# The first stage of layer 0 in another order: X first, modulation blocks in pairs, six projection tiles abreast

## The reference, cut to what matters

```python
mod_l = jnp.split((jax.nn.silu(c) @ ada_w[l] + ada_b[l])[:, None, :], 6, axis=-1)
mod_c = jnp.split(jax.nn.silu(c_ctx) @ ada_w[l] + ada_b[l], 6, axis=-1)
hl = modulate(rmsnorm(xl, norm_mix_pre[l]), mod_l[0], mod_l[1])   # h * (1 + scale) + shift
hc = modulate(rmsnorm(xc, norm_mix_pre[l]), mod_c[0], mod_c[1])
zl = hl @ w_in[l]
zc = hc @ w_in[l]
```

## Time and profile before

| | us |
|---|---|
| median of three runs | 1781.99 (1780.87 to 1786.96) |
| profiled execution | 1783.33 |
| its span | 1781.5 |
| TensorE busy | 1616.1 (91%) |
| VectorE busy | 913.7 (51%) |
| ScalarE busy | 783.3 (44%) |
| GpSimd busy | 302.2 (17%) |

### The profile page before, as it was taken

How to read it: one execution, slowest core, us unless ns; L and a number is a source line. 1 busy time by engine, 2 the same in 40 slices (tenths; PEclk the granted TensorE clock), 3 DMA queues, 4 the chain that set the end, 5 groups by cost and what they waited for, 6 DMA issues and landing times.

```text
span 1781.5 us, 35712 instructions
## 1 busy us (share of the span) xinstructions
PE 1616.1 (91%) x15480; PEld 1325.9 (74%) x15480; DVE 913.7 (51%) x1435; ACT 783.3 (44%) x1286; POOL 302.2 (17%) x241
## 2 busy tenths in 40 slices
PE   3799999977689999799999999899988789979997
PEld 1588767766566668488888886887876678979997
DVE  0444355466335433655555224655676436567754
ACT  1532355564225233634434323624765344565653
POOL 1023023512010000011112100131441110002210
PEclk9799999999899999899999999999999999989999
DMA  8742255504385212123222634734513275425554
GB/s 238 215 145 95 93 180 171 163 17 144 98 269 168 85 47 95 48 95 95 95 95 80 118 96 150 219 120 137 165 58 121 51 256 171 143 95 178 184 159 120
DMA packets 230347, 234.67 MB, mean 132 GB/s; under 512 B 5872, under 2 KB 217072, under 8 KB 230064
## 3 DMA queue, kind: packets, MB, share of 16 engines
q1 hardware_dynamic: 210560, 190.17, 34.0%
q0 software_dynamic: 15024, 35.92, 7.3%
q10 hardware_dynamic: 4608, 6.29, 1.1%
HBM read 216.63 MB, written 15.73 MB: 130 GB/s over the span
## 4 chain that ended last, share of the span: by engine, by line
PE 64%; DVE 5%; issue 5%; ACT 4%; DMA 1%; POOL 0%; ACTq 0%; DVEq 0%; POOLq 0%
PE ps L1792 15%; PE ps L1793 15%; PE ps L1794 15%; PE ps L2136 4%; PE ps L1994 2%; PE ps L1981 2%; PE ps L2033 1%; DVE wlo L1254 1%; PE ps L1830 1%; DVE X L1321 1%; ACT whi L849 1%; PE ps L1955 1%; PE ps L1815 1%; PE ps L1944 1%; DMA ring<-in_ffn_up 1%
## 5 line engine op out<-in xcount | busy, mean ns | idle before, releaser
L849 ACT ACTIVATE whi<-ring 128x1024 fp32r<-128x1024 f32 (+1 forms) x264 | 275.6, 1046 | 566.5 <-PE ps L1794 505.6
L1254 DVE TENSOR_TENSOR wlo<-ring,whi 128x1024 fp32r<-128x1024 f32 (+1 forms) x264 | 327.5, 1244 | 228.3 <-ACT whi L849 227.4
L1792 PE MATMUL ps<-H,whi 128*128 128x512 f32 (+1 forms) x656 | 220.8, 337 | 2.4 <-DVE wlo L1254 2.4
L1793 PE MATMUL ps<-H,whi 128*128 128x512 f32 (+1 forms) x656 | 220.6, 336 | 0.0
L1794 PE MATMUL ps<-H,wlo 128*128 128x512 f32 (+1 forms) x656 | 220.6, 336 | 0.0
L1792 PE MATMUL ps<-HR,whi 128*128 128x512 f32 (+1 forms) x592 | 211.6, 357 | 2.2 <-DVE wlo L1254 1.8
L1794 PE MATMUL ps<-HR,wlo 128*128 128x512 f32 (+1 forms) x592 | 207.7, 351 | 0.0
L1793 PE MATMUL ps<-HR,whi 128*128 128x512 f32 (+1 forms) x592 | 207.7, 351 | 0.0
L1792 PEld LDWEIGHTS ps<-H,whi 128*128 128x128 f32 x656 | 124.6, 190 | 16.0 <-issue 3.2
L1793 PEld LDWEIGHTS ps<-H,whi 128*128 128x128 f32 x656 | 124.6, 190 | 12.7
L1794 PEld LDWEIGHTS ps<-H,wlo 128*128 128x128 f32 x656 | 124.6, 190 | 12.7
(11 more groups left out here) (307 smaller groups left out, 3043.3 us busy)
## 6 DMA issues: line engine op xcount, KB each, us to landing
ring<-in_ada_w SPq DMA_DIRECT2D x48, 1024.0 KB, 5.8
ring<-in_ffn_up SPq DMA_DIRECT2D x44, 1024.0 KB, 5.1
ring<-in_w_gate SPq DMA_DIRECT2D x32, 1024.0 KB, 6.9
ring<-in_w_in SPq DMA_DIRECT2D x24, 1024.0 KB, 5.3
ring<-in_ffn_down SPq DMA_DIRECT2D x32, 512.0 KB, 3.8
WB<-in_w_branch POOLq DMA_DIRECT2D x8, 1024.0 KB, 7.9
ring<-in_w_o SPq DMA_DIRECT2D x8, 1024.0 KB, 5.2
ring<-in_ffn_down SPq DMA_DIRECT2D x16, 384.0 KB, 4.0
```

What stands on the lines that cost most here:

```text
L849: act.activation(whi[:, m % SPLIT, 0:kn, :], ring[:, SLOT[raw] % RING, 0:kn, P * half:P * half + P], ACT.Copy).then_inc(hi_done, 1)
L1254: dve.tensor_tensor(wlo[:, m % SPLIT, 0:kn, :], ring[:, SLOT[raw] % RING, 0:kn, P * half:P * half + P], whi[:, m % SPLIT, 0:kn, :].bitcast ...
L1792: pe.matmul(o[:, c0:c1], hi[:, i, :], part(0, k), start=(k == 0), stop=False)
L1793: pe.matmul(o[:, c0:c1], hi[:, i, :], part(1, k), start=False, stop=False)
```

## The change

- **DMA order.** SP issues c, the first 130 columns of the constants (the ones and `fold`, which now lead the table), X in two halves, modulation blocks 0 and 4, the vectors, three slots of input weights, then blocks 1, 5, 2, 6, 3, 7, then the rest of the constants, and from there on the input weights as before. The eight blocks of the first stage no longer go through `ring`: they have four slots of their own (`ada`) in a part of `Z` that is not used yet. The fifth to eighth of them wait until PE has used the block that lay in their slot.
- **Modulation in pairs.** The jobs are placed by pair: blocks q and 4 + q, then their two transposes, for q = 0 to 3. Pair 0 stands in front of the sum of squares; pairs 1 to 3 stand between the products. DVE makes the gain of two row tiles (`first_gain`) as soon as the pair is there.
- **Six tiles abreast.** `whi` and `wlo` have six slots for the first six tiles of `z`. PE goes over the six tiles for k = 0 and 1, then does pair 1, then k = 2 and 3, and so on; the last two `k` are done tile by tile.
- **ACT and DVE** follow the same order: squares before the first fill, two weight halves, the rows of pair 0, the other four halves, then pair by pair. DVE multiplies all eight row tiles by the root at the first pair. The small vectors and the bias table's addition come after the last pair.
- **Banks.** `NCON_EARLY` is 130, `FIRST` 6, `FIRST_SLOTS` 4. The jobs in front of the first `z` job use banks 6 and 7 in turn, and the counting of banks starts at the first `z` job.

```diff
--- before
+++ after
...
+MOD_FIRST_ORDER = [n for q in range(4) for n in (q, 4 + q)]
...
-    first = modulation_jobs(MOD_FIRST)
-    plan = {("start", 0, 0): first[:5], ("start", 0, 1): first[5:]}
+    plan = {}
+    for q in range(4):
+        pair = [(0, q), (0, 4 + q)]
+        plan["start", 0, q] = [(kind,) + b for kind in ("mod", "modt") for b in pair]
...
     for l in range(LAYERS):
-        jobs += FILL.get(("start", l, 0), []) + [("ss", l, 0)] + FILL.get(("start", l, 1), [])
+        jobs += FILL.get(("start", l, 0), []) + [("ss", l, 0)]
+        for q in range(1, 4):
+            jobs += FILL.get(("start", l, q), [])
         for n, t in enumerate(Z_ORDER):
...
+    early = list(JOB)[:JOB["z", 0, Z_ORDER[0]]]
+    for name in early:
+        k = NBANK - 2 + JOB[name] % 2
+        place[name] = k
+        needs[name] = {owner[k]} - {None}
+        count[k] += 1
+        release[name] = owner[k] = (k, count[k])
...
+        if name in place:
+            continue
...
+        if (l, job[2]) in MOD_FIRST:
+            return []
...
+def half_slot(m):
+    return m if m < FIRST else m % SPLIT
...
+def half_before(m):
+    return m - FIRST if m < FIRST + SPLIT else m - SPLIT
...
-        whi = at("whi", 132, [SPLIT, KT, P], F32R)
-        wlo = at("wlo", 144, [SPLIT, KT, P], F32R)
+        whi_at = [132, 136, 140, 112, 116, 120]
+        wlo_at = [144, 148, 152, 156, 160, 164]
+        whi = [at(f"whi{n}", whi_at[n], [KT, P], F32R) for n in range(FIRST)]
+        wlo = [at(f"wlo{n}", wlo_at[n], [KT, P], F32R) for n in range(FIRST)]
+        ada = at("ada", 48, [FIRST_SLOTS, KT, SLOT_N])
...
+        x_in = [sem("x_in0"), sem("x_in1")]
...
+        ada_in = [sem(f"ada_in{i}") for i in range(FIRST_SLOTS)]
...
         def _(sp):
+            def ada_first(n):
+                o = MOD_FIRST_ORDER.index(n)
+                if o >= FIRST_SLOTS:
+                    sp.wait_ge(mm_done, done_at(("mod", 0, MOD_FIRST_ORDER[o - FIRST_SLOTS])))
+                sp.dma_start(ada[:, o % FIRST_SLOTS, :, :],
+                             a["ada_w"][0, :, n * SLOT_N:(n + 1) * SLOT_N].rearrange("(k p) n -> p k n", p=P))\
+                  .then_inc(ada_in[o % FIRST_SLOTS], 16)
...
+            sp.dma_start(con[:, 0:NCON_EARLY], a["const"][:, 0:NCON_EARLY]).then_inc(const_early, 16)
+            for x in range(2):
+                sp.dma_start(X[:, 4 * x:4 * x + 4, :],
+                             a["xin"][512 * x:512 * x + 512, :].rearrange("(k p) t -> p k t", p=P)).then_inc(x_in[x], 16)
+            ada_first(0)
+            ada_first(4)
+            sp.dma_start(vec[:, :].rearrange("p (l n) -> p l n", l=LAYERS),
+                         a["vecs"].rearrange("l p n -> p l n")).then_inc(vec_in, 16)
...
-                if n == 1:
...
-                    sp.dma_start(con[:, :], a["const"]).then_inc(const_in, 16)
-                if n == 3:
-                    sp.dma_start(X[:, :, :], a["xin"].rearrange("(k p) t -> p k t", p=P)).then_inc(x_in, 16)
-                    sp.dma_start(vec[:, :].rearrange("p (l n) -> p l n", l=LAYERS),
-                                 a["vecs"].rearrange("l p n -> p l n")).then_inc(vec_in, 16)
+                if n == FIRST // 2:
+                    for q in range(1, 4):
+                        ada_first(q)
+                        ada_first(4 + q)
+                    sp.dma_start(con[:, NCON_EARLY:NCON], a["const"][:, NCON_EARLY:NCON]).then_inc(const_in, 16)
...
-                    if m >= SPLIT:
...
-                        old = HALVES[m - SPLIT][0]
+                    if m >= FIRST:
...
+                        old = HALVES[half_before(m)][0]
...
-                            act.wait_ge(mm_done, done_at(HALF_JOB[m - SPLIT]))
...
+                            act.wait_ge(mm_done, done_at(HALF_JOB[half_before(m)]))
...
             def norm_finish(l, k, src, dst):
...
-                act.wait_ge(gains_ready, 2 * l + 1 + k // 2)
+                act.wait_ge(gains_ready, 2 * l + k // 2)
...
-            fill(("start", 0, 0))
-            act.wait_ge(x_in, 16)
...
+                act.wait_ge(x_in[i // 4], 16)
...
+            fill(("start", 0, 0))
...
-            fill(("start", 0, 1))
+            split_until(2)
...
+            def first_rows(i):
+                act.wait_ge(first_gain, i // 2 + 1)
+                act.wait_ge(h_half, i + 1)
+                for x in range(2):
+                    v = Z[:, i, 256 * x:256 * x + 256]
+                    ins = act.activation(v, v, ACT.Identity, bias=mod[:, 0, i, x:x + 1], scale=amod[:, 0, i, x:x + 1])
+                ins.then_inc(h_full, 1)
...
+            def first_high(i):
+                act.wait_ge(h_full, i + 1)
+                act.activation(HR[:, 0, i, :], Z[:, i, :], ACT.Copy).then_inc(h_hi, 1)
...
+            for q in range(4):
+                if q:
+                    fill(("start", 0, q))
+                first_rows(2 * q)
+                first_rows(2 * q + 1)
+                first_high(2 * q)
+                first_high(2 * q + 1)
+                if q == 0:
+                    split_until(FIRST)
             for l in range(LAYERS):
...
-                split_until(half_no(("z", l, Z_ORDER[0])) + SPLIT)
                 if l:
+                    split_until(half_no(("z", l, Z_ORDER[0])) + SPLIT)
...
-                norm_finish(l, 0, Z, HR)
+                    norm_finish(l, 0, Z, HR)
...
                 for n, t in enumerate(Z_ORDER):
...
-                    split_until(half_no(("z", l, t)) + 1 + SPLIT)
+                    split_until(half_no(("z", l, t)) + 1 + (FIRST if l == 0 and n < SPLIT else SPLIT))
...
-                    if (l, k) != (0, 0):
-                        over_rms(l, k, src, tmp, i)
+                    over_rms(l, k, src, tmp, i)
...
-            dve.wait_ge(x_in, 16)
-            for i in range(KT):
-                over_rms(0, 0, X, Z, i)
+            def first_low(i):
+                dve.wait_ge(h_hi, i + 1)
+                dve.tensor_tensor(HR[:, 1, i, :], Z[:, i, :], HR[:, 0, i, :].bitcast(F32), ALU.subtract).then_inc(h_ready, 1)
...
+            for x in range(2):
+                dve.wait_ge(x_in[x], 16)
+            dve.wait_ge(vec_in, 16)
+            for q in range(4):
+                fill(("start", 0, q))
+                gb = vc(0, "mix_pre", 2 * q, 2).unsqueeze(2).to_broadcast([P, 2, 2])
+                for n in (q, 4 + q):
+                    emptied(dve, ("modt", 0, n))
+                dve.scalar_tensor_tensor(amod[:, 0, 2 * q:2 * q + 2, :], mod[:, 0, 8 + 2 * q:10 + 2 * q, :], 1.0, gb,
+                                         ALU.add, ALU.mult).then_inc(first_gain, 1)
+                if q == 0:
+                    for i in range(KT):
+                        over_rms(0, 0, X, Z, i)
+                    split_until(2)
+                first_low(2 * q)
+                first_low(2 * q + 1)
+                if q == 0:
+                    split_until(FIRST)
...
-            dve.wait_ge(vec_in, 16)
             for l in range(LAYERS):
...
-                if l == 0:
-                    fill(("start", 0, 0))
-                    fill(("start", 0, 1))
-                gains(l, (0,))
+                if l:
+                    gains(l, (0,))
...
-                split_until(half_no(("z", l, Z_ORDER[0])) + SPLIT)
-                norm_apply(l, 0, X, Z, HR)
+                if l:
+                    split_until(half_no(("z", l, Z_ORDER[0])) + SPLIT)
+                    norm_apply(l, 0, X, Z, HR)
...
                 for n, t in enumerate(Z_ORDER):
-                    split_until(half_no(("z", l, t)) + SPLIT)
+                    split_until(half_no(("z", l, t)) + (FIRST if l == 0 and n < SPLIT else SPLIT))
...
             def project(name, part, c0, c1, kn=KT, made=None):
...
-                        w = weights(("ada",) + name[1:])
+                        if name[1:] in MOD_FIRST:
+                            n = MOD_FIRST_ORDER.index(name[2])
+                            pe.wait_ge(ada_in[n % FIRST_SLOTS], 16 * (n // FIRST_SLOTS + 1))
+                            w = ada[:, n % FIRST_SLOTS, :, :]
+                        else:
+                            w = weights(("ada",) + name[1:])
...
-                        pe.wait_ge(const_in, 16)
+                        pe.wait_ge(const_early, 16)
...
+            def first_products():
+                names = [("z", 0, t) for t in Z_ORDER[:FIRST]]
+                fill(("start", 0, 0))
+                sum_squares(0, 0, YB)
+                outs = [job(name, JOB[name] - count[0]) for name in names]
+                tiles = []
...
+                def step(k, n):
+                    if n == 0:
+                        pe.wait_ge(h_ready, k + 1)
+                    if k == 0:
+                        tiles.extend(halves(names[n]))
+                    hi, lo = tiles[n]
+                    o = outs[n]
+                    pe.matmul(o, hi[:, k, :], HR[:, 0, k, :], start=(k == 0), stop=False)
```

(51 more changed lines are left out.)

## The result

The median of five runs is 1801.7 us (1795.4 to 1803.79) against 1783.53 (1780.87 to 1788.77) for the kernel before on the same chip: a ratio of 1.0088, 95% interval 1.006 to 1.0116. The change makes the kernel slower by 0.9%, 15.7 us by the ratio. The forecast was 1790.7, 8.7 us more than before; the measured time lies above the stated range. The profiled execution took 1802.23 us, its span is 1800.5.

The account below looks back on a forecast made before the run. PE, 64% of the chain, was taken to bound the kernel: first product 18.9 us earlier, 0.5 lost in the six tiles, 27.0 added by three groups. By the marks 8.7 later: 1792.0 profiled, median 1790.7, range 1781 to 1798.

Parts of the forecast that it names:

- Step 1: Kernel start: block 4 can start at about 24.9, as an earlier block with equal bytes did; sum of squares ends at 38.3.
- S: Time at which PE's sum of squares ends: forecast 38.3, against 45.1 before.
- early bound: Earliest end of the sum of squares, with blocks and some bias reads moving at 346 GB/s: S at 28.9.
- late bound of 41.3: Latest end of the sum of squares, three microseconds later if the weights queued behind cut in.
- Step 2: From the sum of squares to the first product: S + 10.8 = 49.1, against 68.0, 19 us earlier.
- Step 3: Tiles 0 to 5 for k = 0 and 1, waiting for DVE's weight splits: end at S + 20.9 = 59.2.
- Step 4: The three later pairs: blocks 3.1, idle 4.4, products 8.2, clock 1.5, thus 17.2 us each; three take 51.7.
- Step 5: What lies behind the first six tiles: nothing gained or lost, 0, with 2 us either way for the banks.
- the mark: Start of line 1859, the head sums, after the sixth projection tile: 102.22 before, forecast 110.9.
- A: Rival at the kernel's start and groups: data come early and the clock holds, no change, 1781.5; chance 0.2.
- B: Rival at the kernel's start: sum of squares takes half its time, the head start wins, 1776.5; chance 0.08.
- C: Rival in the three groups: PE stays at the low clock level, 27.6 us in all, 1818; chance 0.05.

Follow-up runs that it names:

- e6: The changed kernel with GpSimd's eight bias-table reads issued only when the first normalised row is ready: 1781.06 us, ratio 0.9992 to the kernel before.
- e8: The kernel before the change, with its bias-table reads delayed until the first normalised row: 1773.78 us, ratio 0.9947 to the undelayed one.
- e10: The changed kernel with only the last three of eight bias-table reads waiting for the first normalised row: 1792.56 us, ratio 1.0057 to the kernel before.
- e3: The changed kernel with the DMA of the early constants moved behind blocks 0 and 4: 1799.29 us, ratio 1.007 to the kernel before.
- e4: The changed kernel with 30 unused filler matmuls on PE before the products of each of pairs 1 to 3: 1800.20 us, ratio 1.009 to the kernel before.
- e1: The changed kernel with the next pair's blocks and transposes placed between the two k of a pair's products on PE: 1782.27 us, ratio 0.9988 to the kernel before.
- e7: e5 with the bias-table reads waiting for the first normalised row: 1754.83 us, ratio 0.9849 to the kernel before.
- e5: The changed kernel with e1's edit and the sum of squares in front of the first pair of blocks: 1767.53 us, ratio 0.9914 to the kernel before.

## Why the prediction was wrong

The direction and the mechanism were right: the head start of the first product is less than what three pairs of blocks and their chains, run with PE waiting, cost behind it. The size was not. By its own steps:

- **Step 1 is the one that failed.** It put block 4 at 24.9 "by the row with equal bytes" and S at 38.3. Measured: 31.70 and 44.55, 6.25 us later. Equal bytes in one queue were taken for equal time, though another queue takes a share, and a different one at different times. I had counted the reads' bytes, half of 0.79 MB, at the full rate, which gives 1 us, and put them into the early bound only. What they took was their packets' time: e6 moves block 4 by 15.3 us, of which the row 24.91 held its own part already (in e8 that block starts at 15.80). e10 puts 5.1 of the missing 6.8 on the last three reads, and e3 puts 1.0 on the order of the constants. The rest, 0.7, is not told apart, nor was it tried whether the two add up. The late bound of 41.3 was too low for the same reason: nothing in the earlier trace rows bounded a transfer that shares the engines with another queue, and 3 us were a guess.
- **Step 2** gave S + 10.8 for the first product; measured S + 10.5.
- **Step 3** gave S + 20.9 for the end of k = 1; measured S + 21.3 (65.82). The number came out by luck: it let PE wait for the weight splits and took the low clock level to be hidden by that. PE waits for none (the sixth split is done at 60.16, the product with it starts at 61.40). What set the time are 36 products that ran at the low level for the first 5.0 us.
- **Step 4** gave 17.2 us per group; measured 17.4, 17.3 and 17.3. Its parts: blocks 3.1 (3.1), idle 4.4 (3.9), products 8.2 and the clock 1.5 (together 10.4, so the clock cost 2.2, and 2.0 in the last group). The idle time was put 0.5 too high and the clock's part 0.5 to 0.7 too low, and the two cancel. The fall came in each of the three groups, as counted; e4 confirms the clock's part and e1 the whole.
- **Step 5** gave 0 behind the mark. The shift at the mark, 15.5, stays within 1.3 us to about 1340 us; the profiled execution ends 3.5 us later than that shift. Over all profiled executions the time from mark to end lies between 1673.4 and 1685.9 without an order that follows the edits, so 3.5 is within what it varies by. What makes it vary was not tried.
- **Rivals.** A and B had the data early; e6 and e7 show that they could have been, had the reads not been there. A's ground that the bias reads are out of the way was false: they are issued from 1.3 and 19.0 us on, as before. Its other half, a clock that holds, failed in all three groups. C did not come.

The sum with the measured step 1 is 8.7 + 6.2 = 14.9, against 15.5 at the mark and 15.7 by the ratio.

## What to carry to other kernels

An engine that works in order pays the whole latency of a chain that another pair of engines must run between two of its instructions. Here the start in smaller pieces paid off only once the next piece's first step was issued before the last piece's work, as in e1, and the sum of squares came first: the change with both (e5) is 15 us faster than the kernel before instead of 16 us slower, and either alone is level with it. And before a queue is put in another order, look at the other queues: by the share of the engines' time that they take, not by their bytes.

## What was not expected of the hardware

Eight reads of 96 KB, with rows of 64 values (256 B), took 38.5% of the 16 DMA engines' time over 30 us. Between 5 and 20 us the other queue moved 3.21 MB with them (214 GB/s) and 5.37 MB without them in e6 (358 GB/s). When they are issued decides 16 us of the changed kernel's start. The kernel before had left open whether idle PE keeps its clock for some 2 us or some 5; in the changed one the fall came within 1.5 us of the last transpose in each of the three groups. It took 3.8 to 4.4 us of products to come back, and 5.0 at the first product, where the kernel before had shown about 3.
